# First layer's opening stage of a two-layer hybrid inference step, cut by quarters instead of halves of the model dimension

## The chip, the cores and the metric

The kernel runs on one core of one Trainium2 chip. A core has five engines that run side by side and meet only at semaphores: PE (TensorE, matrix products; its weight loads are shown apart as PEld), DVE (VectorE), ACT (ScalarE), POOL (GpSimd) and SP (SyncE, which here only issues DMAs). All data come from the chip's memory by DMA. The metric is the device time of one execution in microseconds (us); lower is better. Three executions of the kernel before gave 1330.41, 1331.53 and 1332.1 us, so its median is 1331.53.

## What is computed

Two sequences of 128 tokens by 1024 channels (context and latent) go through two trunk layers. All numbers are fp32. The part that matters here is the beginning of layer 0:

```python
sh1, sc1, g1, sh2, sc2, g2 = ada_params(c, w_ada[l], b_ada[l])   # silu(cond) @ w_ada + b_ada
h = modulate(rmsnorm(x, norm1_g[l]), sh1, sc1)                   # rmsnorm(x) * (1 + sc1) + sh1
proj = h @ w_in                                                  # 1024 -> 384 | 256 | 64 | 512
q = rmsnorm(cq, q_norm_g) @ w_uq ;  ckv = rmsnorm(ckv_raw, kv_norm_g)
```

After it come latent attention and a pooling mixer, an output projection, and then a dense SwiGLU (layer 0) or a top-2-of-8 mixture of SwiGLU experts (layer 1). The experts' weights are by far the most of the 471 MB that are read.

## The kernel before, in words

**Layout.** Activations are kept transposed: xT and hT hold 8 blocks (k = 0 to 7) of 128 channels on the partitions, with 256 tokens (128 context, 128 latent) beside each other. Rows of x land in xin by DMA and are transposed on PE (L1808); DVE copies them from PSUM to xT (L1191).

**Precision.** A projection works with split numbers: ACT makes `high` of each weight piece (L851, in `upto`), DVE makes `low`, the rest (L1185), and the activations are split likewise in hx. PE multiplies three times per channel block and output block (L1956, L1957, L1958, in `project_half`).

**The weights' way in.** SP issues the loads in the fixed order of `stream()` into a ring of SLOTS = 7 places (L649 to L690). An item is loaded only when the item 7 places ahead of it has been used up. A second ring of 7 pieces holds high and low. Once layer 1's attention part is done the same memory becomes the experts' ring of 14 places; MOE0, the first multiple of 7 that is not below the number of stream items (110), says which item each of the first 7 loads of the experts must wait for.

**The modulation.** The rows silu(c) @ w_ada are made on PE from items of 1 MB (L1890, in `first_mod_rows`), gathered in one PSUM bank, copied by ACT (L901, in `first_rows`), transposed by PE (L1900, in `turn_first`) and turned into shift and scale by three tiny DVE operations (L1272, L1274, L1278, in `take_first`).

**Halves.** In layer 0 the opening stage goes by two halves of the model dimension. For half 0: four items of w_ada, then three items of w_in. Each half has `first_rows`, `turn_first`, `take_first`, then `norm_b_first` on DVE (L1289, L1295, L1296) for its first two channel blocks and on ACT (L912, L918) for its other two, `lows_of_last` on DVE (L1302), and ten output blocks on PE, each with 12 matmuls of 128x256. The four items of w_ada of half 1 are taken on PE after the output blocks 2 to 5 of half 0, and half 1's `turn_first` after block 6, with three blocks of half 0 still to come. Half 1's weight pieces are split only after its norm.

**Sums of squares.** The norm's factor for layer 0 is made from xT: ACT squares (L867), DVE adds (L1204), PE sums over the partitions (L1844), ACT takes the root (L875), DVE the reciprocal (L1315), and PE spreads it (L1852). DVE then multiplies (`first_normed`, L1263).

**Order at the head of each queue.** PE transposes x first, then the small vectors (biases, gains, the two conditioning vectors; nine small loads issued by ACT), because DVE copies xT before vecT. After `turn_first(0)` PE transposes the cached latents (L1983), for which DVE makes the copies (L1310, L1311), and runs three products of no use to the result (`keep_on`, L1820).

**Behind the stage.** When output block 5 of the last half is done, ACT copies and squares the latents (L936 to L941), DVE adds the squares (L1349, L1351), and PE sums them (L2011) right behind its tenth output block. From there the mixer goes on.

Of the kernel before, what the change touches and what calls it, by code (L numbers as in the profile page):

```python
# [19 lines left out]
D = 1024  # L20
T = 128
DEPTH = 2
PAST = 128
# [117 lines left out]
SUMS = (0, 3, 5, 5, 7)  # L141
# [48 lines left out]
HALF_COLS = ((0, 512), (512, QL + KL + ROPE), (704, 1216))  # L190
HK = KD // 2

HALF_PIECE = (0, 0, 1, 1, 2, 3, 4, 4, 5, 5)
HALF_OFFSET = (0, 128, 0, 128, 0, 0, 0, 128, 0, 128)
HALF_PIECES = 6

IN_LAST, IN_LATENTS = (5, 4), (4, 2)


FIRST_ITEMS = KD // 2  # L200
# [34 lines left out]
def stream():  # L235
# [4 lines left out]
    out = begin[:FIRST_ITEMS] + [("cache", 0, 0)] + [("in", 0, j) for j in range(3)] + begin[FIRST_ITEMS:] + [("in", 0, j) for j in range(3, 6)]  # L240
# [102 lines left out]
def program(nc, ins, consts, y_prompt, y_sample, new_ckv, new_kpe, y_rows):  # L343
# [10 lines left out]
    with ctx:  # L354
# [232 lines left out]
        def shape_of(kind, l, j):  # L587

            if kind == "in" and l == 0:
                return HK, HALF_COLS[j % 3][1] - HALF_COLS[j % 3][0]  # L590
            if kind == "in":
                return KD, IN_COLS[j][1] - IN_COLS[j][0]
            return {"ada": (1, ADA_COLS), "out": (KD, 256), "gate": (KD, FC), "up": (KD, FC), "down": (FC // 128, D)}[kind]

        def raw_piece(n, half):
# [4 lines left out]
            if kind == "in" and l == 0:  # L600
                if j % 3 == 1:
                    return a[:, :, 128:].rearrange("p k (o n) -> p k o n", o=1).to_broadcast([128, k, 2, ROPE]) if half else a[:, :, 0:128]
                return a[:, :, half * 256:(half + 1) * 256]
# [25 lines left out]

        def mod_turned(m):  # L630

            return ps[:, TURNED_BANK[m], :].rearrange("p (q c x) -> p q c x", q=4, c=4)
# [5 lines left out]
        def _(sp):  # L638
# [13 lines left out]
            for n, (kind, l, j) in enumerate(STREAM):  # L652
                if n >= SLOTS:
                    free(sp, n - SLOTS)
                if n == ITEM["in", 0, 5] + 1:
                    sp.dma_start(cst[:, C_ID + 128:], consts[:, C_ID + 128:]).then_inc(consts_in, 16)
# [14 lines left out]
                elif kind == "ada" and l == 0 and j < KD:  # L671
                    half, k = divmod(j, FIRST_ITEMS)
                    to = ring[:, n % SLOTS, :].rearrange("p (k s n) -> p k s n", k=2, s=2)
                    for i in range(2):
                        begin = D * i + 512 * half
                        sp.dma_start(to[:, :, i, :], w["ada"][0][:, 2 * k:2 * k + 2, begin:begin + 512]).then_inc(s, 16)
                elif kind == "in" and l == 0:
                    a, b = HALF_COLS[j % 3]
                    sp.dma_start(slot(n, HK, b - a), w["in"][0][:, j // 3 * HK:(j // 3 + 1) * HK, a:b]).then_inc(s, 16)
# [146 lines left out]
        def _(act):  # L826
# [29 lines left out]

            act.wait_ge(vecT_ready, 1)
# [3 lines left out]
            squared = [0]  # L861
# [8 lines left out]
            def norm_a(t):  # L870

                squares(t, range(squared[0] - 4 * t, 4))
                act.wait_ge(ss_done, t + 1)
                act.wait_ge(cleared, 2)
# [23 lines left out]
            def first_rows(half):  # L898

                act.wait_ge(ada_used, FIRST_ITEMS * (half + 1))  # L900
                A(mrow[:, 1 - half, :], ps[:, ROWS_BANK, :], ACT.Copy).then_inc((rows_first_ready, mrow_ready)[half], 1)  # L901

            def norm_b_first(half):


                act.wait_ge(normed, half + 1)
                act.wait_ge((amod_first_ready, amod_ready)[half], 1)
                x = slice(4 * half + 2, 4 * half + 4)
                for k in (4 * half + 2, 4 * half + 3):
                    for b in range(2):  # L910
                        h = hT[:, k, b * T:(b + 1) * T]
                        last = A(h, h, ACT.Identity, bias=mod[:, 0, k, b:b + 1], scale=amod[:, 0, 0, k, b:b + 1])  # L912
                if half:
# [4 lines left out]
                A(hx[:, x, 0, :], hT[:, x, :], ACT.Copy).then_inc((hxh_first_ready, hxh_ready)[half], 1)  # L918

            norm_a(0)  # L920
            first_rows(0)
            upto(first("in", 0, 0) + 1)
            norm_b_first(0)
            upto(first("in", 0, 0) + HALF_PIECES)
            first_rows(1)
            norm_b_first(1)

            def mixer(l):
# [6 lines left out]
                act.wait_ge(pieces_used, end("in", l, IN_LATENTS[l]))  # L935
# [236 lines left out]
        def _(dve):  # L1172
# [15 lines left out]
            dve.wait_ge(xT_done, 1)  # L1188
            for q in range(2):
                for b in range(2):  # L1190
                    last = V.tensor_copy(xT[:, 4 * q:4 * q + 4, b * T:(b + 1) * T], ps[:, 1 + 2 * b + q, :].rearrange("p (k t) -> p k t", k=4))  # L1191
                last.then_inc(x_ready, 2)
            dve.wait_ge(vecT_done, 1)
            V.tensor_copy(vecT[:, :], ps[:, 0, 0:128 + V_B_ROWS]).then_inc(vecT_ready, 1)
            dve.wait_ge(vecT_ready, 1)

# [68 lines left out]
            def take_first(half):  # L1265


                dve.wait_ge((mod_first_turned, modT_done)[half], 1)
                x = slice(4 * half, 4 * half + 4)
                to = mod[:, 0, 0:16, :].rearrange("p (s r) b -> p r s b", s=2)[:, x, :, :]  # L1270
                bias = vecT[:, V_BADA:V_BADA + 16].rearrange("p (s r o) -> p r s o", s=2, o=1)[:, x, :, :].to_broadcast([128, 4, 2, 2])
                step(V.tensor_tensor(to, mod_turned(0)[:, :, 0:2, 0:2], bias, ALU.add))  # L1272
                done = (mod_first_ready, mod_ready)[half]
                V.tensor_tensor(to, mod_turned(0)[:, :, 2:4, 0:2], to, ALU.add).then_inc(done, 1)  # L1274
                dve.wait_ge(done, 1)
                g = vecT[:, V_N1 + 4 * half:V_N1 + 4 * half + 4].rearrange("p (m o) -> p m o", o=1).to_broadcast([128, 4, 2])
                done = (amod_first_ready, amod_ready)[half]
                V.scalar_tensor_tensor(amod[:, 0, 0, x, :], mod[:, 0, 8 + 4 * half:12 + 4 * half, :], 1.0, g, ALU.add, ALU.mult).then_inc(done, 1)  # L1278
                dve.wait_ge(done, 1)

            def norm_b_first(half):


                dve.wait_ge(normed, half + 1)
                x = slice(4 * half, 4 * half + 2)
                for k in (4 * half, 4 * half + 1):
                    for b in range(2):
                        h = hT[:, k, b * T:(b + 1) * T]
                        last = V.tensor_scalar(h, h, amod[:, 0, 0, k, b:b + 1], mod[:, 0, k, b:b + 1], ALU.mult, ALU.add)  # L1289
                if half:  # L1290
# [4 lines left out]
                step(V.tensor_copy(hx[:, x, 0, :], hT[:, x, :]))  # L1295
                V.tensor_tensor(hx[:, x, 1, :], hT[:, x, :], hx[:, x, 0, :], ALU.subtract).then_inc(hx_begun, 1)  # L1296

            def lows_of_last(half):

                x = slice(4 * half + 2, 4 * half + 4)  # L1300
                dve.wait_ge((hxh_first_ready, hxh_ready)[half], 1)
                V.tensor_tensor(hx[:, x, 1, :], hT[:, x, :], hx[:, x, 0, :], ALU.subtract).then_inc(hx_ready, 1)  # L1302
# [10 lines left out]
            add_squares(0, (1, 2, 3))  # L1313
            dve.wait_ge(rt_ready, 1)
            V.reciprocal(rt[:, :], rt[:, :]).then_inc(rs_ready, 1)  # L1315
            dve.wait_ge(rs_done, 1)
            first_normed(0)
            take_first(0)
            norm_b_first(0)
            upto(first("in", 0, 0) + 1)  # L1320
            lows_of_last(0)
            take_cache(0)
            upto(first("in", 0, 0) + 2)
            first_normed(1)
            upto(first("in", 0, 0) + HALF_PIECES)
            take_first(1)
            norm_b_first(1)
            lows_of_last(1)
# [462 lines left out]
        def _(pe):  # L1791
# [12 lines left out]
            pe.wait_ge(ident_in, 16)  # L1804
            pe.wait_ge(x_router_in, 32)
# [4 lines left out]
            pe.wait_ge(small_in, 16 * 9)  # L1810
            for a, r in ((0, 128), (1, V_B_ROWS)):
                last = nc.tensor.transpose(ps[:, 0, 128 * a:128 * a + r], vrow[0:r, a, :], ident[0:r, 0:r])
            last.then_inc(vecT_done, 1)
# [8 lines left out]
            def norm(t):  # L1822
                if t == 0:
                    pe.wait_ge(vecT_ready, 1)

                pairs = ((0,), (0, 3), (0, 3), (0, 3))[t]
# [53 lines left out]
            def first_mod_rows(items):  # L1880


                for x in items:
                    half, pair = divmod(x, FIRST_ITEMS)
                    if x == FIRST_ITEMS:

                        pe.wait_ge(rows_first_ready, 1)
                    n = arrived("ada", 0, x)
                    for c in range(4):
                        last = mm(ps[32 * c:32 * c + 32, ROWS_BANK, :], silu_c[:, 2 * pair + c // 2, :], ring[:, n % SLOTS, c * ADA_CHUNK:(c + 1) * ADA_CHUNK],  # L1890
                                  start=pair == 0, stop=pair == FIRST_ITEMS - 1, skip_group_check=True)
                    last.then_inc(ada_used, 1)

            def turn_first(half):

                pe.wait_ge((rows_first_ready, mrow_ready)[half], 1)
                if half:
                    pe.wait_ge(mod_first_ready, 1)
# [579 lines left out]
```

## Time and profile before

| what | value |
|---|---|
| median of three executions | 1331.53 us |
| the profiled execution, its own time | 1330.48 us |
| its span in the trace | 1328.7 us |
| mean granted PE clock, share of full | 0.997 |
| PE busy | 1297.7 us, 98% |
| PE weight loads busy | 840.7 us, 63% |
| DVE / ACT / POOL busy | 593.2 / 357.5 / 131.3 us |
| read from memory | 465.43 MB |

The profiled execution is one more execution, 1.05 us below the median; 1.78 us of it lie outside the span. The page of the profile gives whole-span shares; the views by window, by wait and in order of time give the stages. The opening stage takes about the first 60 us of the span. Times of a view count from the span's start.

### The profile page before, as it was taken

What the parts mean: (1) busy time and instruction counts of PE and PEld (TensorE: products, weight loads), DVE (VectorE), ACT (ScalarE), POOL (GpSimd) and SP (SyncE); (2) the same over time, 40 slices, a digit from 0 to 9 for tenths busy, and PEclk for the clock granted to TensorE, in tenths of its full rate; (3) what the DMA queues carried; (4) which work ended last, traced back from release to release, by engine and by line L of the source; (5) the groups of instructions that cost most, each with busy time, mean ns of one, the idle gap of its engine ahead of it and who ended that gap; (6) DMA issues with size and microseconds to landing.
All of it is one profiled execution on the core that took longest, in us unless ns stands there. A gap on an engine that the chain in (4) does not pass through costs nothing.

```text
span 1328.7 us, 28221 instructions
## 1 busy us (share of the span) xinstructions
PE 1297.7 (98%) x12158; PEld 840.7 (63%) x12158; DVE 593.2 (45%) x955; ACT 357.5 (27%) x586; POOL 131.3 (10%) x136
## 2 busy tenths in 40 slices
PE   6999999999999999999999999999999999999996
PEld 4758799998858533456666654545666654556542
DVE  5435755555544514803813732561380381373413
ACT  3334644443434400100700610010160060061001
POOL 0120000000030000000401310000140140131000
PEclk9999999999999999999999999999999999999999
DMA  9999986654693999999999999999999999999991
GB/s 349 361 339 328 359 297 192 192 197 146 259 311 129 421 383 422 384 397 402 421 419 417 420 420 417 420 375 395 408 421 418 419 421 418 417 421 419 417 396 43
DMA packets 113618, 471.41 MB, mean 355 GB/s; under 512 B 10123, under 2 KB 48821, under 8 KB 77654
## 3 DMA queue, kind: packets, MB, share of 16 engines
q1 hardware_dynamic: 111152, 463.80, 88.5%
q10 hardware_dynamic: 1766, 3.70, 0.7%
q8 instruction: 98, 1.61, 0.5%
q0 software_dynamic: 576, 2.10, 0.4%
q14 instruction: 26, 0.21, 0.0%
HBM read 465.43 MB, written 4.13 MB: 353 GB/s over the span
## 4 chain that ended last, share of the span: by engine, by line
PE 92%; DVE 4%; DMA 2%; issue 1%; ACT 1%; POOL 0%; SPq 0%; DVEq 0%; POOLq 0%; ACTq 0%
PE ps L2330 40%; PE ps L2376 18%; PE ps L1917 4%; PE ps L1918 4%; PE ps L1919 4%; PE ps L2345 3%; PE ps L1867 2%; PE ps L1965 2%; DMA token_rows<-y_rows,rti 1%; PE ps L2138 1%; PE ps L2139 1%; PE ps L2140 1%; PE ps L1930 1%; PE ps L1931 1%; PE ps L1932 1%; PE ps L2253 1%
## 5 line engine op out<-in xcount | busy, mean ns | idle before, releaser
L2330 PE MATMUL ps<-ering,xg 128*32 128x512 f32 (+1 forms) x6144 | 585.0, 539 | 1.9 <-DVE sq L1711 1.9
L2330 PEld LDWEIGHTS ps<-ering,xg 128*32 128x32 f32 x6144 | 317.3, 109 | 263.3 <-issue 158.7
L2376 PE MATMUL ps<-ering,eT 128*32 128x512 f32 x1176 | 243.4, 593 | 0.0
L2376 PE MATMUL ps<-wsum,eT 128*32 128x512 f32 x392 | 182.8, 594 | 0.0
L1711 DVE TENSOR_TENSOR sq<-sg,ps 128x512 f32<-128x512 f32 (+1 forms) x48 | 29.7, 619 | 329.3 <-PE ps L2330 245.7
L1121 ACT ACTIVATE sg<-ps 128x512 f32<-128x512 f32 (+1 forms) x48 | 26.1, 544 | 539.0 <-PE ps L2330 539.0
L812 POOL TENSOR_TENSOR sq<-ering 128x512 f32<-128x512 f32 x70 | 96.4, 1377 | 725.3 <-DMA ering<-in_moe_w_down 584.0
L1185 DVE TENSOR_TENSOR low<-ring,high 128x1024 fp32r<-128x1024 f32 (+1 forms) x104 | 122.6, 1202 | 71.5 <-ACT high L851 71.3
L2376 PEld LDWEIGHTS ps<-ering,eT 128*32 128x32 f32 x1176 | 94.4, 110 | 49.1 <-issue 31.7
L1917 PE MATMUL ps<-hx,high 128*128 128x256 f32 x432 | 119.8, 277 | 2.3 <-DVE hx L1239 2.3
L1919 PE MATMUL ps<-hx,low 128*128 128x256 f32 x432 | 119.5, 277 | 0.0
L1918 PE MATMUL ps<-hx,high 128*128 128x256 f32 x432 | 119.5, 277 | 0.0
L851 ACT ACTIVATE high<-ring 128x1024 fp32r<-128x1024 f32 (+1 forms) x104 | 105.0, 1038 | 53.7 <-PE ps L1919 29.1
L1083 ACT ACTIVATE ps<-ering 128x512 f32<-128x512 f32 x190 | 110.5, 600 | 32.3 <-DVE wsum L1589 28.0
L1589 DVE TENSOR_TENSOR wsum<-ps,wsum 128x512 f32<-128x512 f32 x130 | 89.8, 691 | 15.9 <-DVE wsum L1589 12.7
L1917 PEld LDWEIGHTS ps<-hx,high 128*128 128x128 f32 x432 | 81.1, 188 | 4.2 <-issue 4.2
L1918 PEld LDWEIGHTS ps<-hx,high 128*128 128x128 f32 x432 | 81.3, 188 | 0.0
L1919 PEld LDWEIGHTS ps<-hx,low 128*128 128x128 f32 x432 | 81.1, 188 | 0.0
L2376 PEld LDWEIGHTS ps<-wsum,eT 128*32 128x32 f32 x392 | 40.8, 110 | 31.1 <-issue 13.1
L1589 DVE TENSOR_TENSOR wsum<-ering 128x512 f32<-128x512 f32 x38 | 31.5, 828 | 63.2 <-DMA ering<-in_moe_w_down 63.0
L2376 PE MATMUL ps<-wsum,cst 128*32 128x512 f32 x112 | 57.7, 597 | 0.0
L2376 PE MATMUL ps<-ering,sq 128*32 128x512 f32 x112 | 57.2, 592 | 0.0
(295 smaller groups left out, 1622.5 us busy)
## 6 DMA issues: line engine op xcount, KB each, us to landing
ering<-in_moe_w_down SPq DMA_DIRECT2D x112, 1024.0 KB, 13.0
ering<-in_moe_w_gate SPq DMA_DIRECT2D x64, 1024.0 KB, 11.2
ering<-in_moe_w_up SPq DMA_DIRECT2D x64, 1024.0 KB, 13.2
ering<-in_moe_w_gate SPq DMA_DIRECT2D x64, 768.0 KB, 10.2
ering<-in_moe_w_up SPq DMA_DIRECT2D x64, 768.0 KB, 11.6
ring<-in_w_ada SPq DMA_DIRECT2D x40, 1024.0 KB, 7.7
ring<-in_ffn_w_gate SPq DMA_DIRECT2D x11, 1024.0 KB, 6.6
ring<-in_ffn_w_up SPq DMA_DIRECT2D x11, 1024.0 KB, 9.6
```

Of the source, the lines that this page charges most:

```text
L812: nc.gpsimd.tensor_tensor(wdif[:, t % 2, :], b22, b12, ALU.subtract).then_inc(wdif_ready, 1)
L851: A(next(halves(q, raw)), raw, ACT.Copy).then_inc(high_ready, 1)
L1083: A(ps[:, bank, :], (b12, b22, b21)[j], ACT.Copy).then_inc(wcopy_ready, 1)
L1185: V.tensor_tensor(lo, raw, hi, ALU.subtract).then_inc(low_ready, 1)
L1589: V.tensor_tensor(wsum[:, at % W_PLACES, :], x, y, ALU.subtract).then_inc(wsum_ready, 1)
L1711: V.tensor_tensor(hm[:, turn % 2, 0:width], sg[:, g, 0:width], ps[:, UP_BANKS[g], 0:width], ALU.mult).then_inc(eh_ready, 1)
L1917: mm(out, hi[:, k, :], xh, start=n == 0, stop=False)
L1918: mm(out, hi[:, k, :], xl, start=False, stop=False)
L1919: last = mm(out, lo[:, k, :], xh, start=False, stop=n == KD - 1)
L2330: last = mm(ps[32 * c:32 * c + 32, bank, 0:width].rearrange("p (n r) -> p n r", r=64), xg[:, kk, at, 32 * g:32 * g + 32], w[t][:, c, :, :] ...
L2345: last = mm(ps[32 * group:32 * group + 32, bank, :], eT[s][:, g, 2 * i + odd, :], w[:, odd, 512 * half:512 * (half + 1)], start=(s, i) == ...
L2376: last = mm(ps[32 * group:32 * group + 32, bank, :], h, w, start=(n, x) in DOWN_BEGINS, stop=(n, x) in DOWN_ENDS, skip_group_check=True)
```

## The change: what it does

- The opening stage of layer 0 goes by four quarters (two channel blocks each) instead of two halves. An item of w_ada for it now holds four channel blocks of the input and 256 columns each of shift and scale (before: two blocks and 512 columns); two items make one quarter's rows. An item of w_in holds two channel blocks by 640 or 576 columns (before: four blocks by 512, 192 or 512). The stream has 112 items (before 110), with 108 pieces (before 104).
- PE does quarter 0 after two items of w_ada. The two items of the next quarter are taken after output blocks 3 and 6 of the current one, and `turn_first` of the next quarter after block 8, with one block still to come. An output block has 6 matmuls per quarter.
- Each quarter has its own `first_rows`, `turn_first`, `take_first` (now a sum over the four rows' groups, an add and one more operation), norm (one channel block on DVE, one on ACT) and `lows_of_last`. From quarter 1 on the quarter's first weight piece is split before its `first_rows`, the others behind its norm.
- The sums of squares come from xin: two ACT operations over 128x1024 with an accumulated sum, as soon as both loads of x are in; ACT takes the root right after. The operations of L867, L1204 and L1844 fall away for layer 0.
- PE transposes the small vectors ahead of x. DVE copies vecT first and then half of xT; ACT copies the other half.
- The cached latents are loaded first in the ring, transposed ahead of the first rows into another bank, and copied by ACT instead of DVE.

```diff
-FIRST_ITEMS = KD // 2
+FIRST_ITEMS = 2
+QUARTER_COLS = ((0, 640), (640, 1216))
+QUARTER_PIECE = (0, 0, 0, 0, 1, 2, 3, 3, 3, 3)
+QUARTER_WIDTH = (512, 128, 128, 512)
...
-    out = begin[:FIRST_ITEMS] + [("cache", 0, 0)] + [("in", 0, j) for j in range(3)] + begin[FIRST_ITEMS:] + [("in", 0, j) for j in range(3, 6)]
+    out = [("cache", 0, 0)]
+    for quarter in range(QUARTERS):
+        out += begin[FIRST_ITEMS * quarter:FIRST_ITEMS * (quarter + 1)] + [("in", 0, 2 * quarter), ("in", 0, 2 * quarter + 1)]
...
+def latents(l):
+    return end("in", l, IN_LATENTS[l]) + (l == 0)
...
-                    to = ring[:, n % SLOTS, :].rearrange("p (k s n) -> p k s n", k=2, s=2)
+                    to = ring[:, n % SLOTS, :].rearrange("p (k s n) -> p k s n", k=4, s=2)
                     for i in range(2):
-                        begin = D * i + 512 * half
+                        begin = D * i + 256 * quarter
...
+            act.wait_ge(x_router_in, 32)
+            for b in range(2):
+                A(sq[:, 4 * b:4 * b + 4, :].rearrange("p k t -> p (k t)"), xin[:, b, :], ACT.Square, accum_out=stat[:, b:b + 1]).then_inc(sq_ready, 2)
             act.wait_ge(vecT_ready, 1)
             act.wait_ge(cleared, 1)
             A(silu_c[:, :, 0:2]...).then_inc(silu_ready, 1)
+            act.wait_ge(sq_ready, 4)
+            act.wait_ge(cleared, 2)
+            A(rt[:, :], stat[:, 0:2], ACT.Sqrt, scale=1.0 / D, bias=eps[:, 0:1]).then_inc(rt_ready, 1)
+            act.wait_ge(xT_done, 1)
+            for q in range(2):
+                A(xT[:, 4 * q:4 * q + 4, T:2 * T], ps[:, 3 + q, :]..., ACT.Copy).then_inc(x_ready, 1)
+            act.wait_ge(direct_used, DIRECT_USED["cache", 0])
+            A(ckvT[:, :, 2 * T:], ps[:, 5, 0:2 * PAST]..., ACT.Copy)
+            A(kpeT[:, 2 * T:], ps[:, 5, 2 * PAST:3 * PAST], ACT.Copy).then_inc(cacheT_ready, 1)
...
+            for quarter in range(QUARTERS):              # ACT
+                q = first("in", 0, 2 * quarter)
+                if quarter:
+                    upto(q + 1)
+                first_rows(quarter)
+                upto(q + 1)
+                norm_b_first(quarter)
+                upto(q + QUARTER_PIECES)
...
-                act.wait_ge(pieces_used, end("in", l, IN_LATENTS[l]))
+                act.wait_ge(pieces_used, latents(l))
...
+            for quarter in range(QUARTERS):              # DVE
+                q = first("in", 0, 2 * quarter)
+                if quarter:
+                    upto(q + 1)
+                take_first(quarter)
+                norm_b_first(quarter)
+                lows_of_last(quarter)
+                upto(q + QUARTER_PIECES)
+                if quarter == 0:
+                    first_normed(1)
...
+            pe.wait_ge(small_in, 16 * 9)                 # PE
+            for a, r in ((0, 128), (1, V_B_ROWS)):
+                last = nc.tensor.transpose(ps[:, 0, 128 * a:128 * a + r], vrow[0:r, a, :], ident[0:r, 0:r])
+            last.then_inc(vecT_done, 1)
             pe.wait_ge(x_router_in, 32)
...
-            first_mod_rows(range(3))
-            norm(0)
-            first_mod_rows(range(3, 4))
+            turn_cache(0, 5)
+            first_mod_rows(range(1))
+            pe.wait_ge(vecT_ready, 1)
             spread(0)
+            first_mod_rows(range(1, 2))
             turn_first(0)
...
+                    for quarter in range(QUARTERS):
+                        for i, (bank, side) in enumerate(blocks):
+                            if i == 8 and quarter == 0:
+                                pe.wait_ge(cacheT_ready, 1)
+                            project_quarter(quarter, i, bank, side)
+                            if quarter < QUARTERS - 1 and i in (3, 6):
+                                x = FIRST_ITEMS * (quarter + 1) + (i == 6)
+                                first_mod_rows(range(x, x + 1))
+                            if quarter < QUARTERS - 1 and i == 8:
+                                turn_first(quarter + 1)
```

(The three comments naming an engine are added here.) `project_quarter` is `project_half` with two channel blocks; before its first output block it waits for hx_begun (high and low of the quarter's block from DVE) and, for the second channel block, for hx_ready (the block whose high ACT made).

## Rows read from the trace of the kernel before

**Rows 1.** Page, parts 1 and 4: PE's busy time, and the chain by engine.

```profile
PE 1297.7 (98%) x12158; PEld 840.7 (63%) x12158; DVE 593.2 (45%) x955; ACT 357.5 (27%) x586; POOL 131.3 (10%) x136
...
PE 92%; DVE 4%; DMA 2%; issue 1%; ACT 1%; POOL 0%; SPq 0%; DVEq 0%; POOLq 0%; ACTq 0%
```

**Rows 2.** PE's waits behind 480 us (total, times, longest, us).

```profile
PE ps L2330 <- DVE sq L1711: 1.9, 1, 1.9
```

**Rows 3.** Timeline, PE before its first projection (start, length in us, what).

```profile
6.91 3.65 PE L1808 MATMUL ps<-cst,arena 128*128 128x128 f32 x16 [6.91 <-DMA arena<-in_x_sample]
10.35 0.68 PE L1812 MATMUL ps<-cst,arena 128*128 128x128 f32 x2
13.68 4.04 PE L1890 MATMUL ps<-ring,silu_c 128*32 128x512 f32 x24 [2.65 <-issue]
...
19.64 0.71 PE L1852 MATMUL ps<-cst,rt 128*128 128x128 f32 x4
...
21.24 2.74 PE L1820 MATMUL ps<-xT,cst 128*128 128x512 f32 x6
```

**Rows 4.** Timeline, ACT from 5 to 26 us.

```profile
15.67 1.28 ACT L875 ACT_TABLE_LOAD   x1
...
19.77 0.60 ACT L901 ACTIVATE mrow<-ps 128x512 f32<-128x512 f32 x1 [0.76 <-PE ps L1890]
21.06 1.06 ACT L851 ACTIVATE high<-ring 128x1024 fp32r<-128x1024 f32 x1 [0.69 <-DMA ring<-in_w_in]
```

**Rows 5.** DMA packets of ACT's queue that start between 8.75 and 9.0 us.

```profile
q10 hardware_dynamic: 5, 0.00, 2.0%
```

**Rows 6.** Line 676, issues of half items at 3.8 and 4.3 us, and their landing.

```profile
L676 SPq DMA_DIRECT2D ring<-in_w_ada x2: 473/508/544, 3.8 to 4.3; - x2
DMA to landing us min/median/max: 8.4/8.8/9.2
```

**Rows 7.** Timeline, SP's second issue (the load of x_prompt).

```profile
1.20 0.42 SPq L650 DMA_DIRECT2D arena<-in_x_prompt  x1
```

**Rows 8.** Timeline, DVE: the first low piece, ahead of the first projection.

```profile
24.36 1.22 DVE L1185 TENSOR_TENSOR low<-ring,high 128x1024 fp32r<-128x1024 f32 x1
```

**Rows 9.** Timeline, PE in the projection, round rows of modulation, turn and halves.

```profile
29.71 0.28 PE L1958 MATMUL ps<-hx,low 128*128 128x256 f32 x1
...
30.92 0.39 PE L1956 MATMUL ps<-hx,high 128*128 128x256 f32 x1
...
40.10 0.60 PE L1900 MATMUL ps<-cst,mrow 128*128 128x128 f32 x4
40.46 0.37 PE L1956 MATMUL ps<-hx,high 128*128 128x256 f32 x1
...
46.00 0.39 PE L1956 MATMUL ps<-hx,high 128*128 128x256 f32 x1 [1.20 <-DVE low L1185]
```

**Rows 10.** Timeline, DVE between the turned rows and half 1's activations.

```profile
40.74 0.17 DVE L1272 TENSOR_TENSOR mod<-ps,vecT 128x16 f32<-128x16 f32 x1 [8.29 <-PE ps L1900]
...
41.36 1.12 DVE L1289 TENSOR_SCALAR sq<-sq,amod,mod 128x128 f32<-128x128 f32 x4
42.51 0.43 DVE L1295 CAST hx<-sq 128x512 fp32r<-128x512 f32 x1
42.97 0.69 DVE L1296 TENSOR_TENSOR hx<-sq,hx 128x512 fp32r<-128x512 f32 x1
```

**Rows 11.** Timeline, ACT's, DVE's and PE's steps at the end of the stage.

```profile
54.49 0.60 ACT L936 ACTIVATE arena<-ps 128x512 f32<-128x512 f32 x1 [5.92 <-PE ps L1958]
...
58.29 0.43 DVE L1351 TENSOR_TENSOR arena<-arena 128x256 f32<-128x256 f32 x1
...
59.73 0.95 PE L2011 MATMUL ps<-ones,arena 128*128 128x1 f32 x8
```

**Rows 12.** Layer 1's first norm: PE busy, PEld, DVE, ACT, POOL, PEclk, DMA; then PE's timeline.

```profile
330.00:332.00 2.00, 2.00 (x18) 0.43 (x10) 1.96 (x3) 1.23 (x4) 0.00 (x0) 0.58 1.09 331
...
329.41 3.64 PE L1867 MATMUL ps<-ring,silu_c 128*32 128x512 f32 x18
```

More of the change, by code:

```diff
@@ L628, in free, with of_quarter @@
                 eng.wait_ge(low_ready, PIECE0[n + 1])
+        def of_quarter(semaphores, quarter):
+            return (semaphores[0], quarter + 1) if quarter < QUARTERS - 1 else (semaphores[1], 1)
         def mod_turned(m):
@@ L896, in take_rows, with first_rows, norm_b_first @@
                 A(mrow[:, m % 2, :], ps[:, ROWS_BANK, :], ACT.Copy).then_inc(mrow_ready, 1)
[L898 to L913, printed above, removed]
+            def first_rows(quarter):
+                act.wait_ge(ada_used, FIRST_ITEMS * (quarter + 1))
+                if quarter >= 2:
+                    act.wait_ge(mod_first_turned, quarter - 1)
+                done, _ = of_quarter((rows_first_ready, mrow_ready), quarter)
+                A(mrow[:, (quarter + 1) % 2, :], ps[:, ROWS_BANK, :], ACT.Copy).then_inc(done, 1)
+            def norm_b_first(quarter):
+                act.wait_ge(normed, quarter // 2 + 1)
+                act.wait_ge(*of_quarter((amod_first_ready, amod_ready), quarter))
+                k = 2 * quarter + 1
+                for b in range(2):
+                    h = hT[:, k, b * T:(b + 1) * T]
+                    last = A(h, h, ACT.Identity, bias=mod[:, 0, k, b:b + 1], scale=amod[:, 0, 0, k, b:b + 1])
+                if quarter == QUARTERS - 1:
                     last.then_inc(h_last_ready, 1)
@@ L917, in norm_b_first @@
                     step(last)
[L918 to L926, printed above, removed]
+                done, _ = of_quarter((hxh_first_ready, hxh_ready), quarter)
+                A(hx[:, k, 0, :], hT[:, k, :], ACT.Copy).then_inc(done, 1)
+            for quarter in range(QUARTERS):
[6 more added lines that the diff above has]
+                upto(q + QUARTER_PIECES)
             def mixer(l):
@@ L1291, in norm_b_first @@
+            def norm_b_first(quarter):
+                dve.wait_ge(normed, quarter // 2 + 1)
+                k = 2 * quarter
+                for b in range(2):
+                    h = hT[:, k, b * T:(b + 1) * T]
+                    last = V.tensor_scalar(h, h, amod[:, 0, 0, k, b:b + 1], mod[:, 0, k, b:b + 1], ALU.mult, ALU.add)
+                if quarter == QUARTERS - 1:
                     last.then_inc(h_ready, 1)
@@ L1903, in _, with turn_cache @@
-            first_mod_rows(range(3))
-            norm(0)
-            first_mod_rows(range(3, 4))
+                    last = nc.tensor.transpose(mod_turned(0)[:, q, :, :].rearrange("p c x -> p (c x)"), mrow[:, (quarter + 1) % 2, q * 128:(q + 1) * 128], ident)
+                done, _ = of_quarter((mod_first_turned, modT_done), quarter)
+                last.then_inc(done, 1)
+            def turn_cache(l, bank):
+                cache = slot(arrived("cache", l, 0), 3, 128)
+                for m in range(3):
+                    last = nc.tensor.transpose(ps[:, bank, m * 128:(m + 1) * 128], cache[:, m, :], ident)
+                last.then_inc(direct_used, 1)
@@ L1980, in mixer @@
                     pe.wait_ge(x_ready, 4)
[L1981 to L1984 removed]
+                if l:
+                    turn_cache(l, 3)
                 if l == 0:
@@ L2166, in _ @@
                     for m in range(2):
-                        project(half_bank(w, m), first(kind, 0, c) + m, range(KD), 3 if c == 0 and w == 0 and m == 0 else None)
+                        project(half_bank(w, m), first(kind, 0, c) + m, range(KD), 5 if c == 0 and w == 0 and m == 0 else None)
                     if w == 0:
```

173 lines of the change are left out of this document (65 added, 108 removed).

## The prediction, made before the changed kernel was seen to run

> **What bounds the kernel now.** I read the page first: PE is busy 98% of the span and carries 92% of the chain that ended last [rows 1]. Then PE's waits by stage: behind 480 us, where the experts are, the longest is 1.9 us and none is for a DMA [rows 2]. So PE's own work bounds nearly all of the kernel, and a microsecond won or lost on PE in the opening stage comes out at the end, unless something swallows it on the way. Last I read the first 60 us in order of time. PE begins the input projection at 25.63 us (one low piece, 24.36 plus 1.22, and 0.05 of semaphore [rows 8]) and reaches L2011, the sum over the latents' squares, at 59.73 [rows 11]. Everything behind L2011 keeps its order, so the sum is one number: when L2011 starts now.
>
> **The head.** The change has two items of w_ada ahead of the first quarter instead of four. But it also puts the vectors' transposes ahead of x's. Before, x's sixteen ran at 6.91, as soon as x was in [rows 3]. The vectors' nine small loads are issued by ACT, and packets of its queue still start between 8.75 and 9.0 us [rows 5]. I take 9.1 for the last landing. PE is in order, so x's transposes now stand behind it. Step by step:
> - Vectors 9.1 to 9.5, as the second group is issued about 0.4 behind the first of a 0.68 pair. Then sixteen transposes at 3.44 (6.91 to 10.35) [rows 3]: 12.95.
> - Cached latents, three transposes at the pace of x's with a margin: 13.4. They need DVE no more; the two copies go to ACT, which waits then for rows anyway. Nothing on the path.
> - First item of rows. The three items from 13.68 took 4.04 [rows 3], 1.35 each, slower first and 1.0 last; I take 1.7 for the first: 15.1.
> - Spread, 0.7 [rows 3]: 15.8. The root is ready: two ACT squares of 128x1024 at 1.06 each [rows 4] from 6.9 end near 9.3, then at most a table load, silu, a table load (1.28 each [rows 4]) and the root, 12.4.
> - Second item, 1.0 to 1.7, say 1.5: ACT's copy starts at 17.3 (before, 19.77 [rows 4]). Its data: half items issued at 3.8 and 4.3 landed 8.4 and 9.2 us later, at 12.2 and 13.5 [rows 6]. Three small loads now issue ahead at 0.42 each [rows 7], so it lands by about 14, under cover by 1.8 us. Packets of 1 KB instead of 2 KB would have to cost over 10% to show.
>
> From that copy: 0.65 to the turn, 0.64 to DVE (40.10 to 40.74 [rows 9, 10]), three small operations 0.62 (40.74 to 41.36 [rows 10]). Then two of the four multiplies of 1.12 [rows 10], 0.56; a cast of half the size of 0.43, 0.30 with its fixed part; a subtraction of half of 0.69, 0.43; gaps 0.1. DVE now does the lows of ACT's block (0.43) before the first low piece (1.22 [rows 8]). Sum 5.0, so **PE starts at 22.3**, 3.3 earlier. The three idle products, 2.74 [rows 3], end by 21.3 and are covered. Bounds: if the vectors landed with x, all is 2.2 earlier until silu and the root hold it, about 20.2; if PE ran every early product slowly, 23.3.
>
> A rule weighed here: each switch of ACT's function table shows 1.28 us [rows 4] with nothing behind it, and by that the root at 12.4 is 2.7 us ahead of need. The Trainium skill ("ScalarE: Activation LUTs", What ACT_TABLE_LOAD costs) says that a switch also drains the engine and costs about 2.66 us. By that the root would come near 15.1, when spread needs it: no change to my sum, but an early start would be held.
>
> **The projection.** 240 matmuls in all, unchanged. The 120 of the last half ran from 46.00 to 59.73, 0.1144 each [rows 9, 11]: 27.46. Between blocks an item of rows costs PE 1.21 less one matmul's 0.11 (29.71 to 30.92 [rows 9]), and the matmul behind it starts its successor 0.1 late: 1.2. Before four stood there, now **six**: 7.2. A turn costs 0.36 (40.10 to 40.46 [rows 9]): three, 1.1, before one.
>
> **The hand-over between quarters** is what halves paid once and quarters pay three times. From the start of a turn to activations: 0.64 + 0.62 + 0.56 + 0.04 + 0.30 + 0.03 + 0.43 + 0.03 = 2.65 us. PE covers it with the turn, 0.36, and the one block behind it, six matmuls or 0.69. It then stands for **1.6**. The old order had three blocks of twelve behind the turn (4.1 us) and still stood 1.2 ahead of 46.00, for a late low piece [rows 9]; that piece is now split early, which is a true gain, but the cover shrank from 4.1 to 0.7. Three hand-overs: 4.8. Lower bound 0.85 each (smaller tiles with no fixed part, the sum over groups as cheap as the add), upper 1.9 (that sum slow, and the second block's lows late by 0.2).
>
> **The latents.** After block 5 ACT copies and squares and DVE adds, done at 58.72 [rows 11]. Block 5 of the last half ended 72 matmuls behind 46.00, at 54.24: a chain of 4.5 us. Before, four blocks of twelve (5.5 us) covered it. Now four blocks of six are 2.75 us, so PE waits **1.75** at L2011. The rivals for ACT's time do not lengthen it: the quarter's last high piece ends near 1.9 us after its start, block 5 at 4.1.
>
> **Sum.** 22.3 + 27.46 + 7.2 + 1.1 + 4.8 + 1.75 = 64.6 against 59.73: **4.9 us later**.
>
> **The rest, at nothing.** Loads: a quarter has 3.3 MB; at half a MB in 1.3 us (12.2 to 13.5 [rows 6]) that is 8.3 us, and PE's quarter takes 6.9 + 2.4 + 0.4 + 1.6 = 11.3. The ring frees places only as PE goes on, so the DMAs stand idle now and then, but by my estimate each item still lands over 2 us before its use; if that cover went, PE would wait item by item. The constants and the router are issued two places later, still over 10 us ahead of use. The four extra pieces and smaller loads cost SP two more issues of 0.4 us, behind idle time. The experts' first seven loads now wait for other items of layer 1, the first ones for earlier ones; PE waits for no load there [rows 2]. POOL's clearing starts 2.5 us later and is needed after 60 us. DVE loses three additions and half the copies of xT, which lie beside PE's transposes now.
>
> The profiled execution took 1330.48 us and becomes 1335.4; the median is 1.05 above it. **Forecast 1336.4 us.** A measurement of this kernel tells about 0.2%, 2.7 us, from no change.
>
> **The rivals.**
> - *Hand-overs hidden (not slower).* Place: the wait on hx_begun between quarters. Price: three times 1.6. If it were gone the sum is 59.8, the time 1331.6. It decides below 0.87 each, where the loss falls under 2.7. For it: PE's queue runs ahead, DVE's operations shrink. Against: the chain of seven dependent DVE steps is read from rows, and the cover is 1.05. Chance 0.18.
> - *Early start.* The vectors are in with x, PE starts at 20.2: +2.8, 1334.3. The packets at 8.75 [rows 5] speak against it, and the skill's rule above more so. Chance 0.14, split over both sides of the bound.
> - *The landings pace the stage (faster).* If before it was really the weights' landing that set 46.00, then quarters follow the loads: last piece near 44, split by 46 (as half 1's first piece was [rows 9]), 6.9 for the quarter, 1.75 for the latents: 54.6, 5.1 earlier, 1326.4. For it: half 1 did wait for a low piece. Against: PE's own work from 22.3 ends at 58.1 without any wait. It needs rows or turns to be free on PE. Chance 0.12.
> - *PE's clock falls.* Around layer 1's norm, after tiny products and a wait, the granted clock is 0.58 for two us, that is partly at 1.2 GHz, and 18 products took 3.64 us, about 1.5 over the pace of before [rows 12]. The new wait at L2011 with its one-column products is such a place: 1337.9. Chance 0.08.
>
> **How the numbers follow.** Forecast 0.48, from +3.7 to +6.2. Slower by over 0.2%: 0.48 + 0.08 + 0.10 of the early start = 0.66. Within: 0.18 + 0.04 = 0.22. Faster: 0.12. The range goes from 1331.5, just below the hidden hand-overs, to 1338.8, the upper bounds of hand-over and start with part of a clock fall; it leaves out the faster case and little else. The forecast's own range is 1335.2 to 1337.7.
>
> **What would show it.** Right: PE's first projection near 22, x's transposes from 9.5, three idle times of about 1.6 ended by hx lines of DVE, six row items inside the projection, an idle time of about 1.8 at the latents' sum ended by DVE's addition, that sum at 64.6, and the same lengths from there on. Wrong: a start at or below 18, hand-overs under 1 us, PE waits ended by DMAs in the ring, or a distance from the latents' sum to the end that moved by over 1 us, which would mean that my single number is not the whole account.

## The result, and the profile after

The changed kernel takes 1338.31 us in the median of six executions (1335.84 to 1341.27), the kernel before 1331.24 in six beside it (1329.35 to 1332.1). The ratio is 1.0056, with a 95% interval of 1.004 to 1.0071: slower by 7.1 us. The forecast was 4.9 us slower, or 1336.4, with 1338.8 as the upper end of the range. The profiled execution took 1339.22 us, span 1337.4, which is 8.7 above the span before. Of the executions of two experiments below, three took 1519 to 7767 us, and their medians are those of the others.

The page, part 1 of it, for the changed kernel:

```profile
PE 1302.4 (97%) x12158; PEld 841.2 (63%) x12158; DVE 593.7 (44%) x964; ACT 362.6 (27%) x599; POOL 131.0 (10%) x136
```

PE has as many matmuls as before [rows 1] and is busy 4.7 us longer: the same work at a slower pace somewhere. The rest of the 8.7 us is idle time. PE's waits up to 80 us say where (total, times, longest, us):

```profile
PE ps L1834 <- DMA arena<-in_kv_norm_g: 8.8, 1, 8.8
PE ps L1987 <- DVE hx L1324: 4.5, 3, 1.5
PE ps L2040 <- DVE arena L1378: 1.5, 1, 1.5
PE ps L1987 <- DVE low L1215: 1.1, 1, 1.1
PE ps L1925 <- ACT mrow L930: 0.7, 1, 0.7
```

The first row is the head: PE now waits for the last small vector. The second is the hand-over, three times 1.50 us, each ended by DVE's lows of its own block. The third is the wait for the latents. The fourth is the start of the projection, where PE waits for DVE's first low piece. None but the first is ended by a DMA. In order of time, PE in the head and one hand-over (start, length, us):

```profile
8.84 0.71 PE L1834 MATMUL ps<-cst,arena 128*128 128x128 f32 x2 [8.84 <-DMA arena<-in_kv_norm_g]
9.48 3.67 PE L1839 MATMUL ps<-cst,arena 128*128 128x128 f32 x16
...
17.97 2.74 PE L1847 MATMUL ps<-xT,cst 128*128 128x512 f32 x6
...
21.84 0.39 PE L1987 MATMUL ps<-hx,high 128*128 128x256 f32 x1 [1.13 <-DVE low L1215]
...
30.50 0.60 PE L1925 MATMUL ps<-cst,mrow 128*128 128x128 f32 x4
...
33.30 0.36 PE L1987 MATMUL ps<-hx,high 128*128 128x256 f32 x1 [1.50 <-DVE hx L1324]
```

The projection starts at 21.84 instead of 25.63, and each quarter takes 11.5 us (21.84, 33.30, 44.78, 56.28). The chain that PE waits for, on DVE, in the first hand-over:

```profile
31.13 0.19 DVE L1299 TENSOR_REDUCE stat<-ps 128x8 f32<-128x32 f32 x1 [4.32 <-PE ps L1925]
...
31.76 0.60 DVE L1317 TENSOR_SCALAR sq<-sq,amod,mod 128x128 f32<-128x128 f32 x2
32.40 0.29 DVE L1323 CAST hx<-sq 128x256 fp32r<-128x256 f32 x1
32.73 0.42 DVE L1324 TENSOR_TENSOR hx<-sq,hx 128x256 fp32r<-128x256 f32 x1
```

Against [rows 10] each step has half the data, but the three small steps ahead take as long as before: 0.63 us from 31.13 to 31.76. The turn began at 30.50 and the activations were there at 33.15, 2.65 us, while PE had 1.1 us to do.

Behind the projection, PE again:

```profile
65.11 1.39 PE L2040 MATMUL ps<-ones,arena 128*128 128x1 f32 x8 [1.49 <-DVE arena L1378]
66.36 0.78 PE L2044 MATMUL ps<-arena,cst 128*128 128x128 f32 x2
67.06 6.30 PE L1892 MATMUL ps<-ring,silu_c 128*32 128x512 f32 x32
...
76.60 5.45 PE L1996 MATMUL ps<-arena,ring 128*128 128x256 f32 x24 [0.29 <-DVE arena L1401]
```

L2040 is the old L2011, at 65.11 instead of 59.73 [rows 11]: **5.4 us later**. But the query projection behind it starts at 76.60, where the kernel before had 67.81: 8.8 later. Of the 3.4 us between, 2.7 are in the 32 products of rows, 6.30 us for what took 3.64, and 0.7 in the small products ahead of them. The stretches there, with the granted clock behind the five engines' busy times:

```profile
64.00:66.00 2.00, 0.89 (x7) 0.90 (x7) 1.97 (x4) 0.00 (x0) 0.00 (x0) 0.91 0.03 12
66.00:68.00 2.00, 2.00 (x13) 1.12 (x16) 1.19 (x4) 0.42 (x2) 1.59 (x3) 0.50 0.00 0
68.00:70.00 2.00, 2.00 (x16) 0.51 (x12) 1.08 (x3) 0.00 (x0) 1.84 (x5) 0.50 0.00 0
70.00:72.00 2.00, 2.00 (x12) 0.40 (x8) 0.00 (x0) 0.00 (x0) 1.92 (x4) 0.50 1.00 246
```

At 0.50 PE is granted 1.2 GHz, for 6.8 us in all, and it loses half of them. From 76.60 on the distance to the end is 1260.8 us, and 1260.9 in the kernel before; in the profiles of the experiments it goes from 1259.9 to 1263.6, so that so close an agreement is partly chance. For this pair the profile splits 8.7 into 5.4 of stage and 3.4 of clock. Whether the second part belongs to the change, the experiments had to say.

### The profile page after: what moved, and what is told of

It reads as the page before. It is cut to its first block, busy times and chain, and to the rows that moved or that the text cites. A ratio compares the mean times of both kernels' runs of the same rounds, so it can differ in the third digit from the quotient of the medians.

```text
span 1337.4 us, 28255 instructions
## 1 busy us (share of the span) xinstructions
PE 1302.4 (97%) x12158; PEld 841.2 (63%) x12158; DVE 593.7 (44%) x964; ACT 362.6 (27%) x599; POOL 131.0 (10%) x136
## 4 chain that ended last, share of the span: by engine, by line
PE 91%; DVE 4%; DMA 2%; ACT 1%; issue 0%; ACTq 0%; POOL 0%; DVEq 0%; POOLq 0%
PE ps L2359 40%; PE ps L2405 18%; PE ps L1951 4%; PE ps L1952 4%; PE ps L1953 4%; PE ps L2374 3%; PE ps L1892 2%; PE ps L1996 2%; DMA token_rows<-y_rows,rti 1%; PE ps L2168 1%; PE ps L2167 1%; PE ps L2169 1%; PE ps L1964 1%; PE ps L1965 1%; PE ps L1966 1%; PE ps L2282 1%
```

## The experiments

In each the time is compared with runs of the kernel before on the same chip. Line numbers of kernels made from the changed one are its own, shifted by at most two.

**1. turn_early: more cover for the hand-over.**

```diff
-                            if quarter < QUARTERS - 1 and i in (3, 6):
-                                x = FIRST_ITEMS * (quarter + 1) + (i == 6)
+                            if quarter < QUARTERS - 1 and i in (1, 4):
+                                x = FIRST_ITEMS * (quarter + 1) + (i == 4)
...
-                            if quarter < QUARTERS - 1 and i == 8:
+                            if quarter < QUARTERS - 1 and i == 6:
```

> The changed kernel with each quarter's two items of rows taken after output blocks 1 and 4 instead of 3 and 6, and the next quarter's turn after block 6 instead of 8, so that three blocks (2.1 us) instead of one (0.7 us) stand behind it. Theory (the chain of DVE steps behind the turn is the hand-over, and its cover is too short): the three idle times of 1.50 us ended by DVE's hx shrink to 0.1 to 0.3 each, the latents' sum starts near 61.2 instead of 65.1, the time falls by 4 us. Rival (the landings of the weights pace the quarters): the idle times stay near 1.5 in sum and are ended by a low or high piece instead.

Measured: 1332.55 us in the median of nine, beside 1331.77 for the kernel before; ratio 1.0007 (0.9993 to 1.0021). PE's waits:

```profile
PE ps L2040 <- DVE arena L1378: 1.6, 1, 1.6
PE ps L1987 <- DVE low L1215: 1.1, 1, 1.1
```

The row of three waits for hx is gone altogether, though the same weights arrive through the same queue. The items of rows also free their places in the ring earlier here, so this run alone does not rule the landings out; the next one, which moves the turn only, does. The sum starts at 60.98 (65.11 in the changed kernel), and the median lies 5.8 us below the changed kernel's. Moving three small groups of instructions by two blocks takes back most of the loss.

**2. turn_late: no cover.**

```diff
-                            if quarter < QUARTERS - 1 and i == 8:
+                            if quarter < QUARTERS - 1 and i == 9:
```

> The changed kernel with the next quarter's turn after block 9, the last, instead of 8: nothing covers the chain. Theory: each of the three idle times grows by the one block, 0.69 us, to 2.2, and the latents' sum moves from 65.1 to 67.2. Rival (landings pace the quarters): unchanged at 1.5.

One execution: 1341.01 us. The waits:

```profile
PE ps L1987 <- DVE hx L1324: 6.6, 3, 2.2
```

Three times 2.20, as the theory has it: one block less of cover is one block more of wait, with every load as before. The chain behind the turn sets the hand-over, and the landings do not. But the sum starts at 71.06 and not at 67.2. Stretches around the three hand-overs (PE, PEld, DVE, ACT, POOL, clock, DMA) say why:

```profile
33.00:36.00 3.00, 2.38 (x11) 2.41 (x12) 2.47 (x6) 2.95 (x6) 0.00 (x0) 0.57 1.07 367
...
48.00:50.00 2.00, 2.00 (x12) 2.00 (x11) 1.54 (x3) 1.62 (x2) 0.00 (x0) 0.50 0.63 127
...
62.00:64.00 2.00, 2.00 (x11) 2.00 (x11) 1.23 (x1) 0.31 (x1) 0.00 (x0) 0.50 0.79 209
```

With each of the three waits of 2.2 us PE's clock went to 1.2 GHz for a time; with the waits of 1.5 us in the changed kernel it never did. The expectation had the wait right and missed this second price, which came to about 4 us.

**3. fill_idle: PE kept busy in the latents' wait.**

```diff
+                if l == 0:
+                    keep_on(0, 3, 256, moving=xT[:, :, :].rearrange("p k t -> p (k t)"))
                 pe.wait_ge(sqqk_added, 2 * l + 2)
```

> The changed kernel with three idle products of 256 columns (about 1.4 us of PE, no use to the result) between the projection's end and the latents' sum. Theory (the wait of 1.5 to 2 us together with the one-column products behind it lets PE's clock fall, 6.8 us at 1.2 GHz in the profile): the sum still starts near 65.1, the clock stays at 2.4 GHz there, the 32 row products behind it take 3.6 us instead of 6.3, and the time falls by 3 us on average. Rival (the clock falls for another reason, for instance the three waits between quarters or the later start): the fall stays at about the same place.

Measured: 1335.84 us in the median of ten, ratio 1.0031 (1.0021 to 1.004): 4.1 us above the kernel before beside it, where the changed kernel was 7.1 above its own. PE around the sum:

```profile
63.25 1.46 PE L1847 MATMUL ps<-xT,cst 128*128 128x256 f32 x6
64.89 1.05 PE L2042 MATMUL ps<-ones,arena 128*128 128x1 f32 x8 [0.19 <-DVE arena L1378]
65.81 0.47 PE L2046 MATMUL ps<-arena,cst 128*128 128x128 f32 x2
66.20 3.64 PE L1892 MATMUL ps<-ring,silu_c 128*32 128x512 f32 x32
```

The sum starts where it did, and the rows take 3.64 us again. Products that compute nothing did not slow the kernel, and by these medians, taken at different times, made it 3.0 us faster, for which the clock is the only reason that the profile offers. The 3.64 by itself proves little: experiments 1, 2, 5 and 6 have it too, with the wait left as it was.

**4. late_latents: the same wait put into the kernel before.**

```diff
-                act.wait_ge(pieces_used, end("in", l, IN_LATENTS[l]))
+                act.wait_ge(pieces_used, end("in", l, IN_LAST[l] if l == 0 else IN_LATENTS[l]))
```

> The kernel before with one wait moved: ACT takes layer 0's latents behind output block 9 instead of block 5, so that their chain of 4.5 us has no cover. Theory (waits at the latents' sum cost their length, and let PE's clock fall): the sum starts 4.5 us later, near 64.3, and in most executions the clock falls to 1.2 GHz within the next few us for 3.4 us or more, so the time grows by 4.5 plus 1.5 to 3.4, to 1337.5 to 1339.5. Rival (the clock's fall belongs to the quarters): +4.5 alone, 1335.8.

Measured: 1339.02 us in the median of four, ratio 1.0051 (1.0034 to 1.0067): 7.3 us above the kernel before beside it, where the rival had 4.5. PE and the clock:

```profile
65.12 1.86 PE L2011 MATMUL ps<-ones,arena 128*128 128x1 f32 x8 [4.31 <-DVE arena L1351]
```

```profile
66.00:68.00 2.00, 2.00 (x11) 1.52 (x15) 0.72 (x3) 0.41 (x2) 1.58 (x3) 0.50 0.00 0
68.00:70.00 2.00, 2.00 (x12) 0.40 (x8) 1.58 (x4) 0.00 (x0) 1.84 (x5) 0.50 0.02 4
```

A kernel by halves shows the same picture, with the sum at nearly the same time: a fall at the sum needs no quarters. The wait is longer here, 4.3 us against 1.5. The sum starts 5.4 us later than before instead of 4.5, for the head ended 0.3 later and the last half's matmuls took 0.119 each instead of 0.114 in this profile. That leaves 1.9 of the 7.3 for the clock by the medians, less than the interval is wide; the profile itself shows the fall, and 3.3 us from the sum to the query projection (11.3 for 8.1).

How often a wait of 1.5 us there brings it is another matter. Of the five profiles with that wait (the changed kernel, turn_early, turn_late, x_first, x_first_bare) only the changed kernel's shows a fall at the sum. So 3.4 us is what one execution paid, and the mean price is not settled. The changed kernel's median gives 7.1 - 5.4 = 1.7, and its loss less that of fill_idle 3.0. Measured together, turn_early lies 3.3 us below fill_idle with the sum 3.9 earlier, and x_first 1.8 above it with the sum 1.5 later: a price of 0.6 and 0.3. The mean granted clock of all executions leans to the higher figures, 0.9937 to 0.9940 with the wait (the changed kernel, turn_early, x_first) and 0.9954 to 0.9961 with it filled (fill_idle, early_fill, split_first); but the kernel before, which has no such wait, had 0.9944 to 0.9952 beside them. Falls come elsewhere too in some executions and not in others: six of the eleven profiles have one of 3.4 us between 132 and 150 us, among them fill_idle's and late_latents', and neither the kernel before's nor the changed kernel's.

**5. x_first: the head in the old order.**

```diff
+            pe.wait_ge(x_router_in, 32)
+            ...sixteen transposes of x...
             pe.wait_ge(small_in, 16 * 9)
             ...two transposes of the vectors...
-            pe.wait_ge(x_router_in, 32)
-            ...sixteen transposes of x...
```

> The changed kernel with x's transposes ahead of the small vectors' on PE again, everything else as changed. Theory (the head is held by the vectors' landing near 8.8, with silu at 11.7 next): the transposes begin near 6.9, the first rows near 11.7 instead of 13.7, the projection near 19.9 instead of 21.8, the time falls by 2 us. Rival (the second item of rows or the root holds the head): the projection still starts within 0.5 us of 21.8.

Measured: 1337.6 us in the median of eight, ratio 1.0039 (1.0028 to 1.0051): no gain clear of the changed kernel's interval. Both expectations were wrong:

```profile
6.66 3.65 PE L1835 MATMUL ps<-cst,arena 128*128 128x128 f32 x16 [6.66 <-DMA arena<-in_x_sample]
...
11.72 0.88 PE L1933 MATMUL ps<-cst,ring 128*128 128x128 f32 x3 [0.94 <-POOL arena L783]
12.53 1.94 PE L1915 MATMUL ps<-ring,silu_c 128*32 128x512 f32 x8
...
19.11 3.98 PE L1847 MATMUL ps<-xT,cst 128*128 128x512 f32 x6
```

ACT ahead of the rows:

```profile
11.39 0.23 ACT L876 ACTIVATE silu_c<-vecT 128x16 f32<-128x16 f32 x1
```

PE first stood for 0.94 us. The row names POOL, but what PE waits for there in the kernel, and had not yet got, is silu, done at 11.62: with the vectors out of the way ACT holds the head next, as the theory had it. The first item of rows did begin 1.2 us earlier, but it took 1.94 us instead of the usual 1.06, and the three idle products 3.98 instead of 2.74. They ended at 23.0 and held the projection until 23.02, 1.2 us later than in the changed kernel. The clock's column shows 1.00 there, but only because the trace has no record of the granted clock before 21.6 us. The lengths tell that PE ran at half pace until then.

**6. x_first_bare: the same without the idle products.**

```diff
-                if l == 0:
-                    keep_on(1, 3, moving=xT[:, :, :].rearrange("p k t -> p (k t)"))
```

> As x_first (x's transposes ahead of the small vectors'), and without the three idle products behind the first turn. Theory (in x_first the early products ran at half pace, so that the idle products took 4 us and held the projection's start at 23.0): the projection starts near 22.4 when DVE's low piece is ready, with its first matmuls at half pace. Rival (something else held it): it starts at 23.0 as before.

One execution: 1336.74 us. The projection starts at 20.28, earlier than expected, since this time the rows took 1.06 each. But PE had then stood for 3.75 us:

```profile
20.28 0.52 PE L1987 MATMUL ps<-hx,high 128*128 128x256 f32 x1 [3.75 <-DVE low L1215]
20.60 0.42 PE L1988 MATMUL ps<-hx,high 128*128 128x256 f32 x1
20.82 0.41 PE L1989 MATMUL ps<-hx,low 128*128 128x256 f32 x1
```

The matmuls start 0.21 apart instead of 0.11, until 23.6 us: the clock is 0.58 from 20 to 22. That gives back 1.5 us of the head's gain, and the sum starts at 65.20, as in the changed kernel. The wait that the idle products fill is the likely reason: before it PE ran at full pace. So an earlier head bought nothing in either form. Why x_first's head ran slowly and this one's did not, in the same order of work, the records tell in part: the first record of the granted clock, at full, lies at 21.6 us there, at 10.1 here and at 14.5 in the changed kernel, and PE's products get shorter where it begins. Why it came so late in x_first stays unexplained: each is one profile.

**7. head_only: the new head on the kernel by halves.** The sums of squares from xin, vecT first, the cached latents first in the ring; everything by halves.

```diff
-    out = begin[:FIRST_ITEMS] + [("cache", 0, 0)] + [("in", 0, j) for j in range(3)] + begin[FIRST_ITEMS:] + ...
+    out = [("cache", 0, 0)] + begin[:FIRST_ITEMS] + [("in", 0, j) for j in range(3)] + begin[FIRST_ITEMS:] + ...
...
-            first_mod_rows(range(3))
-            norm(0)
-            first_mod_rows(range(3, 4))
+            turn_cache(0, 5)
+            first_mod_rows(range(3))
+            pe.wait_ge(vecT_ready, 1)
             spread(0)
+            first_mod_rows(range(3, 4))
```

> The kernel before, by halves, with the changed head alone: sums of squares from x's rows on ACT, small vectors transposed first, cached latents loaded first and copied by ACT. Theory (the head's gain came from waiting for two items of rows instead of four, not from the squares): ACT's copy of the first rows starts within 0.6 us of 19.77 and the projection within 0.8 us of 25.6, the time is that of the kernel before within 1 us. Rival (the sums of squares on PE and DVE held the head): the projection starts near 23.5 and the time falls by 2 us.

Measured: 1331.56 us in the median of ten, ratio 0.9996 (0.9986 to 1.0005). ACT's copy of the rows starts at 19.78 (19.77 before) and the projection at 25.24 (25.63). PE now waits for the fourth item:

```profile
18.65 1.06 PE L1895 MATMUL ps<-ring,silu_c 128*32 128x512 f32 x8 [1.00 <-DMA ring<-in_w_ada]
```

So the new head by itself gains nothing while four items are needed, and the 3.8 us come from needing two. What the squares from x's rows would gain if the fourth item were there in time is not shown: it now lands 1.0 us too late, with the cached latents loaded ahead of it.

**8. early_fill: both repairs, with useful work in the wait.** The edits of turn_early, and:

```diff
+                beside = items_at("latents", l)
+                if l == 0:
+                    mod_rows(beside[:2])
                 pe.wait_ge(sqqk_added, 2 * l + 2)
...
-                beside = items_at("latents", l)
-                mod_rows(beside[:len(beside) - 4])
+                mod_rows(beside[0 if l else 2:len(beside) - 4])
```

> The changed kernel with both repairs that are useful work: the rows after blocks 1 and 4 and the turn after 6 (as in turn_early), and the first two items of rows of the next modulation group taken by PE between the projection's end and the latents' sum instead of behind it. Theory (three hand-overs and the latents' wait are the whole loss, the clock's fall follows from the wait): no idle time over 0.3 us in the projection, none at the sum, no fall of the clock near 65 us, and against turn_early another 1.6 us gone from the point where the query projection starts: 1331 us, or 0.5 to 1 below the kernel before. Rival (the two items that are missing behind the sum are then missed there): the idle time moves behind the sum, before the spread, and the time is that of turn_early, 1332.8.

Measured: 1330.12 us in the median of eleven, beside 1331.75; ratio 0.9989 (0.998 to 0.9998). The two items fill the wait and are not missed behind it:

```profile
59.24 1.92 PE L1892 MATMUL ps<-ring,silu_c 128*32 128x512 f32 x16
61.09 1.05 PE L2043 MATMUL ps<-ones,arena 128*128 128x1 f32 x8
```

The query projection starts at 67.56, where turn_early had 69.16 and the kernel before 67.81.

**9. split_first: the last wait of the head.** early_fill, and:

```diff
                 q = first("in", 0, 2 * quarter)
-                if quarter:
-                    upto(q + 1)
+                upto(q + 1)
```

on ACT and on DVE.

> early_fill with quarter 0 treated as the others: its first weight piece is split (high on ACT, low on DVE) before its first rows are copied, instead of behind its norm. Theory (the head now ends with the low piece behind the activations' lows, 1.65 us that DVE and ACT could have done while they waited for rows): the projection starts near 20.8, when the three idle products end, instead of 22.2, and the time falls by 1.2 us against early_fill, to 1329. Rival (that piece of w_in has not landed when ACT would split it, so that ACT's copy of the rows is late by as much): ACT's copy of the first rows moves from 16.8 to 17.5 or later and the start stays at 22.2.

Measured: 1329.56 us in the median of eleven, beside 1332.2 for the kernel before; ratio **0.9979 (0.997 to 0.9988)**, clear of 1 and 8.8 us below the changed kernel's median. The piece had landed: ACT waited for it only 0.3 us (until 15.18), and the rows' copy began at 16.36. The projection starts at 19.86, 0.9 earlier than expected, as soon as the idle products let it, and DVE's low piece is no longer among PE's waits. Quarters in this order beat the kernel before. That they are the better cut is not shown, for the kernel before also waits for low pieces, 2.8 us in two waits:

```profile
PE ps L1956 <- DVE low L1185: 2.8, 2, 1.6
```

It was not run with those pieces split earlier, and up to as much as the 2.6 us gained here might lie there.

## Why the prediction came out as it did

**Direction and main mechanism: right.** Slower by over 0.2% had 0.66 of the chance. The median, 1338.31, lies in the range but 0.6 above the forecast's own range (1335.2 to 1337.7). The stage's sum was forecast at +4.9 and was +5.4:
- *Head:* forecast start 22.3, measured 21.84. The vectors' landing held PE until 8.84 (taken: 9.1), and the two items of rows took 1.40 and 1.06, not 1.7 and 1.5; ACT's copy began at 16.83, not 17.3.
- *Hand-over:* forecast 1.6 each; the idle rows say 1.50, which count from the modelled end of the last matmul. Matmuls follow each other every 0.11 us, though each is shown 0.28 long; counted from 0.11 behind the last one's start, as the forecast did, the wait is 1.67. The chain took 2.65 us, exactly as summed. Experiments 1 and 2 show it from both sides: no wait with three blocks of cover, 2.2 with none.
- *Quarters:* three periods of 11.2 by the forecast's terms, 11.5 measured: 0.7 us, from the slower first matmuls behind each wait and turn and the hand-overs' tenths. The last quarter took 7.2 instead of 6.9.
- *Latents:* 1.75 forecast; the idle row says 1.49, and counted from 0.11 behind the last matmul's start (63.34) to 65.11 it is 1.66. The head's 0.5 too late and the quarters' 1.0 too short make up the difference of 0.5: part of the agreement is errors that cancel.
- *Loads at nothing:* right. No PE wait up to 80 us ends on a ring's DMA, and the experts' stage has the length it had.

**The term that was mis-sized: PE's clock.** "PE's clock falls" stood among the rivals with a chance of 0.08 and a price of 1.5 us, taken from one fall of 3.4 us at layer 1's norm [rows 12]. The wait and the place were named rightly. What failed is the step "everything behind L2011 keeps its order, so the sum is one number": the order was kept and the pace was not. The distance from the sum to the end grew by 3.3 us (1269.0 to 1272.3), which the prediction itself had put down as a sign of being wrong. The price was mis-sized as well, for it took the fall at layer 1's norm as the measure. At the sum the fall lasted 6.8 us and cost 3.4 in the profiled execution; in the mean it cost something between 0.3 and 3.0, and which is open. That the time fell inside the range is owed in part to its upper end, where part of a clock fall had been let in.

**The rivals.** Landings that pace the stage: refuted by turn_late, and turn_early agrees. Early start: the packets at 8.75 spoke truly, and x_first shows that even the early start gains nothing, first through silu behind ACT's two switches (0.94 us), then through PE's pace. The table switches cost 1.28 us each and nothing more, here in the changed kernel:

```profile
10.13 1.28 ACT L876 ACT_TABLE_LOAD   x1
11.43 0.23 ACT L876 ACTIVATE silu_c<-vecT 128x16 f32<-128x16 f32 x1
```

So the measurement decides against the drain that the Trainium skill gives ("ScalarE: Activation LUTs", What ACT_TABLE_LOAD costs). There was one more of them than before, ahead of silu, and it was hidden as assumed.

## What to carry to other kernels

Cutting a stage finer brings its start forward once, but it pays every hand-over again and shrinks the cover of each: count the dependent small operations between two parts, which don't get shorter with the tile, and put that many microseconds of the old part behind the point where the new one is begun. Look also at what drained in the shadow of the last part, since a shorter last part hides less. The finer cut is worth having only with its order of work remade: here two lines moved by two blocks, two items of independent work put into the wait, and one piece split earlier turned 7 us of loss into 2.6 us of gain. Whether the coarse cut with the same repairs would have done as well was not tried.

## What the hardware showed that was not expected

- Waits of PE can cost twice, by their length and by the clock behind them: dense matmuls with waits of 1.5 us kept 2.4 GHz in all twelve hand-overs of four profiles, with 2.2 us they lost it three times out of three (experiment 2), and a wait of 4.3 us before one-column products brought 6.8 us at 1.2 GHz (experiment 4).
- The profile's clock column reads 1.00 wherever the trace has no record. In all profiles here the first record comes at 10 to 22 us, and where an item of rows falls ahead of it, as in x_first, it takes 1.94 us instead of 1.06. At the head of a kernel the lengths tell the pace, and the column does not.
- A Square with a sum over 1024 columns on ACT took 1.06 us, and the read of its accumulator 0.19, half hidden; its being the first operation of the program, ahead of silu, costs one switch of the table more.
